# Layer-0 attention of a two-layer diffusion backbone: query roots as token columns in the exponential's scale, rotary halves swapped by ScalarE copies, square sums in column bands

## The reference

```python
def _rmsnorm(x, g):
    xf = x.astype(F32)
    y = xf * lax.rsqrt(jnp.mean(xf * xf, axis=-1, keepdims=True) + EPS)
    return (y * g.astype(F32)).astype(x.dtype)

def _rope(x, cos, sin):
    half = x.shape[-1] // 2
    x1, x2 = x[..., :half], x[..., half:]
    return jnp.concatenate([x1 * cs - x2 * sn, x2 * cs + x1 * sn], axis=-1)

q, k, v, hy, gate = _split(u_lat @ w_in, EVEN_SPLIT)
q = _rope(_rmsnorm(_heads(q, A_HEADS), qn_g), *rope_h)
k = _rope(_rmsnorm(_heads(k, A_KV_HEADS), kn_g), *rope_h)
# softmax over [window keys, context keys, sink] of q.k * HEAD_DIM ** -0.5, then times v, times silu(gate)
```

## Time and profile before

| | us |
|---|---|
| median of 3 runs | 1658.29 |
| lowest, highest | 1656.76, 1664.85 |
| profiled execution, its own time | 1660.79 |
| its span, first to last instruction | 1659.0 |
| PE busy | 1547.5 (93%) |
| DVE busy | 1028.8 (62%) |
| ACT busy | 566.1 (34%) |

### The profile page before, as it was taken

The page is one execution under the profiler, slowest core; times in us unless marked ns, Lnnn a source line. Parts: engine busy times, 40 slices in busy tenths (PEclk is TensorE's granted clock), DMA queues, the critical chain, the costliest instruction groups (busy, mean ns, idle before and its releaser), DMA issues. The chain is left out here.

```text
span 1659.0 us, 19427 instructions
## 1 busy us (share of the span) xinstructions
PE 1547.5 (93%) x7827; PEld 1213.0 (73%) x7827; DVE 1028.8 (62%) x1174; ACT 566.1 (34%) x787; POOL 212.2 (13%) x226
## 2 busy tenths in 40 slices
PE   4996899999999999999999899978999988999998
PEld 1333578888887868877877688866788866788998
DVE  3253389888988766677775545444657556565543
ACT  1333312222222223332222311136337555454432
POOL 0000033232322100000000144420000000000000
PEclk9988899999999999999999899979999999999999
DMA  9467565454645634444356666632232222232464
GB/s 348 145 235 279 206 246 190 155 197 145 213 149 169 219 102 152 160 136 146 118 200 212 232 217 220 226 148 76 77 128 102 87 79 96 64 106 105 168 222 144
DMA packets 66859, 274.41 MB, mean 165 GB/s; under 512 B 10897, under 2 KB 19281, under 8 KB 46033
## 3 DMA queue, kind: packets, MB, share of 16 engines
q1 hardware_dynamic: 46306, 195.56, 33.6%
q0 software_dynamic: 20464, 77.60, 13.9%
HBM read 256.36 MB, written 16.78 MB: 165 GB/s over the span
## 5 line engine op out<-in xcount | busy, mean ns | idle before, releaser
L984 PE MATMUL banks<-xh,wh 128*128 128x512 f32 (+1 forms) x1840 | 638.2, 363 | 16.5 <-ACT wh L944 4.8
L987 PE MATMUL banks<-xl,wh 128*128 128x512 f32 (+1 forms) x1840 | 620.9, 353 | 0.3 <-DVE xl L1762 0.2
L984 PEld LDWEIGHTS banks<-xh,wh 128*128 128x128 f32 x1840 | 351.8, 191 | 69.4 <-issue 17.2
L987 PEld LDWEIGHTS banks<-xl,wh 128*128 128x128 f32 x1840 | 351.6, 191 | 54.6 <-issue 5.3
L990 PE MATMUL banks<-xh,wl 128*128 128x512 f32 (+1 forms) x1840 | 360.8, 349 | 0.0
L954 DVE TENSOR_TENSOR wl<-raw,wh 128x2048 fp32r<-128x2048 f32 (+1 forms) x124 | 281.8, 2273 | 106.8 <-ACT wh L944 106.8
L990 PEld LDWEIGHTS banks<-xh,wl 128*128 128x128 f32 x1840 | 301.0, 189 | 44.2
L944 ACT ACTIVATE wh<-raw 128x2048 fp32r<-128x2048 f32 (+1 forms) x124 | 235.4, 1899 | 252.7 <-PE banks L990 162.5
L365 DVE SCALAR_TENSOR_TENSOR ada_acc<-ada_w,cond,ada_acc 128x1024 f32<-128x1024 f32 x120 | 159.5, 1329 | 6.5 <-DMA ada_w<-in_ada_rest 4.4
L388 POOL DMA_DIRECT2D ada_w<-in_ada_rest x128 | 70.2, 549 | 629.1 <-DVE ada_acc L377 404.8
L377 DVE SCALAR_TENSOR_TENSOR ada_acc<-ada_w,cond,ada_acc 128x1024 f32<-128x1024 f32 x90 | 126.4, 1404 | 0.0
(11 more groups left out here) (271 smaller groups left out, 1639.4 us busy)
## 6 DMA issues: line engine op xcount, KB each, us to landing
ada_w<-in_ada_rest POOLq DMA_DIRECT2D x128, 512.0 KB, 3.9
raw<-in_ev_tiles SPq DMA_DIRECT2D x52, 1024.0 KB, 6.0
raw<-in_od_tiles SPq DMA_DIRECT2D x34, 1024.0 KB, 4.8
ada_ring<-in_ada_first SPq DMA_DIRECT2D x32, 1024.0 KB, 6.4
raw<-in_out_tiles SPq DMA_DIRECT2D x32, 1024.0 KB, 5.2
hT<-in_hT POOLq DMA_DIRECT2D x4, 1024.0 KB, 25.5
spectra<-kstage POOLq DMA_DIRECT2D x8, 512.0 KB, 8.3
kf<-spectra SPq DMA_DIRECT2D x4, 1024.0 KB, 4.8
```

Source lines behind the costliest of these rows:

```text
L984: nc.tensor.matmul(out, wh[:, k, :], b.xh[:, seg, k, :], start=(k == 0), stop=False)
L987: nc.tensor.matmul(out, wh[:, k, :], b.xl[:, seg, k, :], start=False, stop=False)
```

## The change

1. **Root out of the queries.** Queries are no longer divided by their root. ACT drains a query tile straight into `qk` with the gain as the copy's scale, and DVE rotates it unnormalised. The root, which belongs to a query's token, goes into the exponential: `scale` there becomes a column `qscale` (one value for each query token, on the partitions of the score bank), and the row maximum's negative is scaled by `nqscale`, in two operations of one column in the place of one of two.
2. **Key root spread by its own sum.** The key's squares are summed with a full matrix of ones (r = 1), so that every partition has the sum; ACT takes the root at r = 2, DVE reciprocal and product at r = 3 (`scale_key`). No `pick` is left.
3. **Column bands.** The four query sums go, each as a matmul of 32 output rows, into a band of 32 partitions of bank 7, two behind tile r = 4 and two behind r = 6. ACT copies the bank to `sq` at r = 6; at r = 7 PE transposes it in four pieces (`square_columns`); ACT takes the root of 16 columns (`rq`), DVE makes `qscale` and `nqscale` (`query_scales`).
4. **Halves swapped by copies.** ACT copies 64 partitions of the bank's 256 latent columns to the other half of `qsw`, twice per tile. DVE multiplies by a swapped gain and the sine, the tile by the cosine, and adds: three operations of 256 columns, at once behind the drain of the tile (r = 0, 2, 3, 4, 5) and no more at r = 7. `swap` is gone.
5. `qk` gets a buffer for each head (in the place of `pre`), and `load_mixed(0)` waits for the last scores of head 0 (`scored` 8) in the place of `normed` 10.

```diff
@@ PE
-                nc.tensor.matmul(ps[7], b.batch[:, 112 - 16 * j:240 - 16 * j], b.sq[:, n % 2, :],
-                                 start=(j == 0), stop=(j == 4)).then_inc(s.ssq_mm, 1)
+                    nc.tensor.matmul(ps[7], b.ones, b.sq[:, n % 2, :], start=True, stop=True).then_inc(s.ssq_mm, 1)
+                    return
+                pe.wait_ge(s.rs_step, 3 * kv + 1)
+                nc.tensor.matmul(ps[7][32 * j - 32:32 * j, :], b.ones[:, 0:32], b.sq[:, n % 2, :], start=True, stop=True,
+                                 skip_group_check=True).then_inc(s.ssq_mm, 1)
...
+            def square_columns(kv):
+                pe.wait_ge(s.rs_step, 3 * kv + 2)
+                pe.wait_ge(s.vtok_ready, kv + 1)
+                if kv:
+                    pe.wait_ge(s.probT_ready, 8)
+                for c in range(4):
+                    last = nc.tensor.transpose(ps[4][:, c * P:(c + 1) * P], b.sq[:, 0, c * P:(c + 1) * P], b.ident)
...
-                    if 3 <= r <= 6:
+                    if r in (4, 6):
+                        sum_squares(kv, r - 3)
                         sum_squares(kv, r - 2)
...
                 if 0 <= kv < KV and r == 7:
-                    normalise(kv)
+                    square_columns(kv)
@@ ACT
-                    a.activation(b.pre[:, j, :], bank, ACT.Copy).then_inc(s.kept, 1)
+                    if j:
+                        act.wait_ge(s.vT, kv + 1)
                     if n >= 2:
-                        act.wait_ge(s.ssq_mm, n - 1)
+                        act.wait_ge(s.roped, n - 1)
+                    for half in range(2):
+                        here, there = (slice(64 * h, 64 * h + 64) for h in (half, 1 - half))
+                        a.activation(b.qsw[here, n % 2, :], bank[there, 0:256], ACT.Copy).then_inc(s.kept, 1)
+                    gain = COL["ev_qn"] if j else COL["ev_kn"]
+                    a.activation(b.qk[kv][:, j, :], bank, ACT.Copy, scale=b.cols[:, gain:gain + 1]).then_inc(s.kept, 1)
...
                     a.activation(b.prob[:, q, 0:keys], ps[2 + q][:, 0:keys], ACT.Exp, bias=b.nb[:, q:q + 1],
-                                 scale=SCALE_H, accum_out=b.rowsum[:, q:q + 1]).then_inc(s.exped, 1)
+                                 scale=b.qscale[:, kv, at:at + 1], accum_out=b.rowsum[:, q:q + 1]).then_inc(s.exped, 1)
...
+                if 0 <= kv < KV and r == 2:
+                    a.activation(b.rs[:], ps[7], ACT.Sqrt, scale=1.0 / HD, bias=b.small[:, 0:1]).then_inc(s.rs_step, 1)
                 if 0 <= kv < KV and r == 6:
-                    a.activation(b.rs[:], ps[7], ACT.Sqrt, scale=1.0 / HD, bias=b.small[:, 0:1]).then_inc(s.rs_root, 1)
+                    a.activation(b.sq[:, 0, :], ps[7], ACT.Copy).then_inc(s.rs_step, 1)
+                if 0 <= kv < KV and r == 7:
+                    a.activation(b.rq[:], ps[4].rearrange("p (c j w) -> p j c w", c=4, j=4)[:, :, :, 0], ACT.Sqrt,
+                                 scale=1.0 / HD, bias=b.small[:, 0:1]).then_inc(s.rs_step, 1)
@@ DVE
+            def rope(kv, j):
+                dve.wait_ge(s.kept, 3 * n + 3)
+                v.scalar_tensor_tensor(out=swapped, in0=swapped, scalar=b.cols[:, gain:gain + 1], in1=b.sh, op0=ALU.mult,
+                                       op1=ALU.mult).then_inc(s.rope_sin, 1)
+                v.tensor_tensor(lat, lat, b.ch, ALU.mult).then_inc(s.rope_cos, 1)
+                v.tensor_tensor(lat, lat, swapped, ALU.add).then_inc(s.roped, 1)
+            def scale_key(kv):
+                v.reciprocal(b.rs[:], b.rs[:]).then_inc(s.rs_ready, 1)
+                v.tensor_tensor(b.qk[kv][:, 0, :], b.qk[kv][:, 0, :], b.rs[:], ALU.mult).then_inc(s.normed, 1)
+            def query_scales(kv):
+                v.reciprocal(rq, rq).then_inc(s.rs_ready, 1)
+                v.tensor_scalar(b.qscale[:, kv], rq, SCALE_H, None, ALU.mult).then_inc(s.rs_ready, 1)
+                v.tensor_scalar(b.nqscale[:, kv], rq, -SCALE_H, None, ALU.mult).then_inc(s.rs_ready, 1)
...
-                v.tensor_scalar(b.nb[:], b.mx[:], -SCALE_H, b.nsink[:, head:head + 1], ALU.mult, ALU.min).then_inc(
-                    s.nb_ready, 1)
+                for q in range(2):
+                    v.tensor_scalar(b.nb[:, q:q + 1], b.mx[:, q:q + 1], b.nqscale[:, kv, at:at + 1],
+                                    b.nsink[:, head:head + 1], ALU.mult, ALU.min).then_inc(s.nb_ready, 1)
...
-                if 0 <= kv < KV and r == 6:
-                    v.reciprocal(b.rs[:], b.rs[:]).then_inc(s.rs_ready, 1)
+                if 0 <= kv < KV and r in (0, 2, 3, 4, 5):
+                    rope(kv, r - 1 if r else 0)
+                if 0 <= kv < KV and r == 3:
+                    scale_key(kv)
+                if 0 <= kv < KV and r == 7:
+                    query_scales(kv)
@@ SP, load_mixed(0)
-        sp.wait_ge(s.normed, 10)
+        sp.wait_ge(s.scored, 8)
```

More of the change, by code:

```diff
@@ L73, in vector_rows @@
           twice(a["od_mk_g"][:, HD:]))
-    place(2, 0, a["c"], a["c_ctx"], *(twice(a[n]) for n in ("hy_b1", "hy_f1", "hy_b2", "hy_f2")))
+    place(2, 0, a["c"], a["c_ctx"], *(twice(a[n]) for n in ("hy_b1", "hy_f1", "hy_b2", "hy_f2")),
+          *(np.roll(a[n], HD // 2, axis=-1) for n in ("ev_qn_g", "ev_kn_g", "od_qn_g", "od_kn_g")))
     mlpw = np.zeros((64, 384), np.float32)
@@ L274, in sbuf_map @@
     b.odd = put("odd", "S", 44 * K, [P, 2, 2, P])
-    b.pre = put("pre", "S", 4 * K, [P, 5, T])
     b.sq = put("sq", "S", 0, [P, 2, T])
-    b.qk = put("qk", "S", 14 * K, [P, 5, T])
+    b.qk = [put(f"qk{kv}", "S", (4 + 10 * kv) * K, [P, 5, T]) for kv in range(KV)]
+    b.rq = put("rq", "V", 2560, [P, GROUP, 4])
+    b.qscale = put("qscale", "V", 2624, [P, KV, GROUP * 4])
+    b.nqscale = put("nqscale", "V", 2752, [P, KV, GROUP * 4])
     b.vtok = put("vtok", "S", 24 * K, [P, 2, 4, HD])
@@ L509, in _ @@
             nc.tensor.transpose(ps[6][:, 128:238], b.rows[0:110, 1, :], b.ident[0:110, 0:110])
-            nc.tensor.transpose(ps[6][:, 238:274], b.rows[0:36, 2, :], b.ident[0:36, 0:36]).then_inc(s.colsT, 1)
+            nc.tensor.transpose(ps[6][:, 238:278], b.rows[0:40, 2, :], b.ident[0:40, 0:40]).then_inc(s.colsT, 1)
             nc.tensor.matmul(ps[2][0:64, 0:256], b.w1, b.zpos, start=True, stop=True).then_inc(s.mlp_mm, 1)
@@ L1177, in v_transposes @@
                 last.then_inc(s.vT, 1)
[L1179 to L1209, removed]
+            def square_columns(kv):
+                pe.wait_ge(s.rs_step, 3 * kv + 2)
+                pe.wait_ge(s.vtok_ready, kv + 1)
+                if kv:
+                    pe.wait_ge(s.probT_ready, 8)
+                for c in range(4):
+                    last = nc.tensor.transpose(ps[4][:, c * P:(c + 1) * P], b.sq[:, 0, c * P:(c + 1) * P], b.ident)
+                last.then_inc(s.ssq_mm, 1)
             def scores(u):
@@ L1214, in scores @@
                 pe.wait_ge(s.roped, 5 * (kv + 1))
+                pe.wait_ge(s.normed, kv + 1)
+                if u == 0:
+                    pe.wait_ge(s.mixed, 16)
                 if u > 0:
@@ L1218, in scores @@
                     at = 256 * part + P * q
-                    lhs = b.qk[:, 1 + head, at:at + P]
+                    lhs = b.qk[kv][:, 1 + head, at:at + P]
                     if part == 0:
-                        nc.tensor.matmul(ps[2 + q], lhs, b.qk[:, 0, :], start=True, stop=False)
+                        nc.tensor.matmul(ps[2 + q], lhs, b.qk[kv][:, 0, :], start=True, stop=False)
                         far = slice(P * (1 - q), P * (2 - q))
@@ L1225, in scores @@
                     else:
-                        last = nc.tensor.matmul(ps[2 + q][:, 0:256], lhs, b.qk[:, 0, 256:512], start=True, stop=True)
+                        last = nc.tensor.matmul(ps[2 + q][:, 0:256], lhs, b.qk[kv][:, 0, 256:512], start=True,
+                                                stop=True)
                 last.then_inc(s.scored, 1)
@@ L1357, in exps @@
                 head, keys = 4 * kv + n // 2, 512 - 256 * (n % 2)
-                act.wait_ge(s.nb_ready, u + 1)
+                act.wait_ge(s.nb_ready, 2 * u + 2)
+                act.wait_ge(s.rs_ready, 4 * kv + 4)
                 if u > 0:
@@ new lines, in rope @@
+            def rope(kv, j):
+                n = 5 * kv + j
+                lat = b.qk[kv][:, j, 0:256]
+                swapped = b.qsw[:, n % 2, :]
+                gain = COL["ev_qn_sw"] if j else COL["ev_kn_sw"]
+                if n == 0:
+                    dve.wait_ge(s.core_in, 96)
+                dve.wait_ge(s.kept, 3 * n + 3)
+                v.scalar_tensor_tensor(out=swapped, in0=swapped, scalar=b.cols[:, gain:gain + 1], in1=b.sh, op0=ALU.mult,
+                                       op1=ALU.mult).then_inc(s.rope_sin, 1)
+                v.tensor_tensor(lat, lat, b.ch, ALU.mult).then_inc(s.rope_cos, 1)
+                dve.wait_ge(s.rope_sin, n + 1)
+                dve.wait_ge(s.rope_cos, n + 1)
+                v.tensor_tensor(lat, lat, swapped, ALU.add).then_inc(s.roped, 1)
```

(3 more changed lines are left out.)

84 lines of the change are left out of this document (32 added, 52 removed).

## The result

The changed kernel took 1642.49 us in the median of four runs (1638.18 to 1646.74), the kernel before 1659.88 in the median of four (1656.76 to 1664.85). The ratio is 0.9894, with a 95% interval from 0.9855 to 0.9932. That is 17.4 us less. The forecast was 19.3 us less than before. Its 1639.0 us lies 3.5 us under the measured median: 1.6 us of that is the kernel before, whose median of four is that much above the 1658.29 that the forecast started from, and 1.9 us is the change itself. The measured median lies in the range of 1632 to 1650.

The account below looks back on a forecast made before the run. TensorE, busy 93% of the span, was taken as the bound. Terms -19.7 + 0.9 - 2.6 + 2.1 = -19.3 us gave 1641.5 from the profiled 1660.79, or 1639.0 us from the median 1658.29; range 1632 to 1650.

Parts of the forecast that it names:

- the first rival: Square sums: two bands run one behind the other, costing +0.9 in the place of -2.6 us; time 1642.5; 6%.
- Normalise leaves TensorE: Behind tiles 31 and 41: TensorE's normalise block is on the path in full, so removing it gives -19.7 us.
- Transposes: Four transposes of the sums behind each of tiles 31 and 41: +0.9 us for two heads.
- Square sums: Ten full sums become two full ones and four pairs of bands that run side by side: -2.6 us.
- VectorE's new places: Rotations at r = 0, 2, 3, 4, 5 and key scaling at r = 3 fit VectorE's idle time: nothing.
- ScalarE's new work: Half copies, roots and table loads at r = 2 and r = 7 fit ScalarE's idle time before drains: nothing.
- Slower exponential: Pointer scale and two nb operations add 0.35 us a unit; six units in tiles 44 to 49 show it: +2.1 us.
- Earlier load at tile 43: load_mixed(0) no longer waits for head 1's scaling; TensorE did not wait for that weight, so nothing.
- late VectorE: At r = 3 VectorE's turn outruns its cover and TensorE waits for wl: -2.3 us in total, 1656; 4%.
- the chain in series: Drain, copies, rotation and next split stand between products in ten tiles: +34 us, +14.7 net, 1673; 3%.
- the clock in the gate stage: Three more turns lose 1.7 us each to a lower clock, loop at its upper end: -12.7 in total, 1645.6; 13%.
- Everything hidden: The loop's extra cost finds slack and bands change at no cost: -22.2 us in total, 1636.1; 8%.

Follow-up runs that it names:

- the kernels with and without the load first: SP's load_mixed moved behind the next weight load, in the kernel before and in the changed kernel: medians 1650.63 and 1631.1 us, gate stages 99.80 and 99.81 us.

## Why the prediction was right

The mechanism was right in its large term and in the loop that gives part of it back. Of the 1.9 us by which the change falls short of the forecast's 19.3, 1.2 are a wait on ScalarE that the prediction put at nothing and 0.3 the size of a band. Two agreements are luck. The measured median of 1642.49 is the time of the first rival, 1642.5, though the bands do overlap. And the loop's term came out within 0.2 us in a stage that scatters by 1 us either way.

*Normalise leaves TensorE: -19.7.* Right. Measured by leaving it out: 19.7. In the changed kernel the two gaps fell by 9.66 + 9.13 = 18.8, which with the transposes' 0.9 is 19.7 again.

*Transposes: +0.9.* Measured 0.44 for head 0's, and no wait for ScalarE's copy. The prediction named a wait for ScalarE at the transposes as a sign of being wrong. At these there is none; the one that came stands at the probabilities' transposes, and is the step on ScalarE below.

*Square sums: -2.6.* The mechanism was right and the size off. A full sum costs 0.90, a pair 1.22, so 2 x 0.90 + 4 x 1.22 - 10 x 0.90 = -2.3. The rows that I read the change of width from had four bands and a full-width fp32 matmul behind them. Head 1's pairs have one behind them too, and there the first matmul behind starts 0.98 us after the pair (698.19 to 699.17), 0.12 over a full sum's 0.86; behind head 0's, where a product follows, it is 1.09, 0.23 over. With the 0.1 us ahead of the pair that makes 0.2 in head 1, as forecast, and 0.3 in head 0.

*VectorE's new places: 0.* Right. The turn at r = 3 ran without a gap into the next, as forecast, and `wl` was in time. The rotation's first two operations took 0.50 and 0.53 in the mean, not 0.42.

*ScalarE's new work: 0.* This step failed at one place. I counted ScalarE's idle time and the bank behind the drain, and did not ask who waits for the operation behind the drain. V's copy at tile 36 came late by 0.96 us, and the stretch lost 1.2 us by it. The idle time before a drain says nothing about an operation after it.

*Slower exponential: +2.1.* Right in mechanism and place, and in size as far as the scatter lets one tell. Measured +2.24 in the one profile and +1.9 in the mean of four profiles each; the +2.2 from the kernels with and without the load first rests on the same first profiles and is no third measurement. The unit's price was 0.41, not 0.35, since the second `nb` operation took its full 0.23.

*Earlier load at tile 43: 0.* 42 to 44 kept its length.

The sum of the measured terms is -19.7 + 0.9 - 2.3 + 1.2 + 2.2 = -17.7 us, and from tile 24 to the next block the profile shows -17.8, the medians -17.4. Most of the terms are read from the same profile, so the first agreement says only that no stretch was left out. Of the rivals, bands without overlap, late VectorE and the chain in series are out. So is the clock in the gate stage as a cost of the change: no further turn lost clock, the stage lost 3.4 us to it before and 3.4 after, and TensorE's busy time in it stayed the same. Everything hidden is out with the 2.3 us of longer waits.

## What to carry to other kernels

Read what a block costs on the bound engine as the distance between the work on either side, not as a sum of waits: here that came out to the tenth. When an operation gets slower, follow its chain through the DMA queue as well: a transfer that stands behind a wait ties its neighbours to that wait, and moving one small load behind the big one shortened the stage by 8.7 us in one kernel and by 11.0 in the other (6.4 and 11.4 in the medians). And when operations are added ahead of one on an engine with idle time, ask for each operation behind them who is waiting for it.

## What was not expected of the hardware

- A band of 32 output columns costs TensorE as much as two side by side, 1.22 us, and more than one full-width matmul of the same 512 columns, 0.90 us. The Trainium skill, page TensorEngine Tiling (Array Packing), Key Properties, says that changing the mode drains TensorE; the 0.3 us agree with it, but whether the drain is all of them no run here shows.
- A wait of 3.8 us for `wh` cost more than itself: the granted clock fell to 0.71 over 8 us, partly at the 1.2 GHz level, and the stage gained 11.0 us when 7.1 us of waits were taken away. The length of the wait alone does not say whether the clock falls: behind a wait of 2.5 us at 880 us of the same profile it stayed at 1.00, and behind one of 1.8 us at 900 us of the kernel before it fell to 0.79.
- The gate stages without the queue's wait agree to 0.01 us across five kernels, while with it eight profiles of six kernels of nearly the same work scatter from 107.4 to 111.9. What made the stage scatter was the loop through the transfers, and the clock with it: TensorE's busy time in the eight lies between 102.3 and 104.0 us, where it is 99.8 without the queue's wait. What the transfers themselves vary by was not tried.
